# Sums of squares behind the next scores, value rows scaled last, and three PSUM banks in turn for values and tiles

## The chip, the cores and the metric

One core of a Trainium2 chip runs the program; the others are idle. The time is the device time of one execution in microseconds. Less is better.

## What is computed

Two transformer blocks on 1024 rows of width 1024, in float32. Only the first block's projections and attentions matter here; the gates, the feed-forward layer and the whole second block stay as they are.

```python
h = rms_norm(x, norm_mix[l])
aq, ak, av, bq, bk, bv, cq = jnp.split(h @ w_in[l], offsets, axis=-1)
aq = rms_norm(aq.reshape(b, t, A_HEADS, 2, A_HEAD_DIM), a_q_norm[l])
ak = rms_norm(ak.reshape(b, t, A_HEADS, 2, A_HEAD_DIM), a_k_norm[l])
...
out_a = diff_attention(aq, ak, av, slopes_a, lam)   # p[0] - lam * p[1], times v
out_a = (rms_norm(out_a, a_subln[l]) * (1.0 - lambda_init)).reshape(b, t, BRANCH_WIDTH)
...
out_c = memory_attention(cq, ck, cv)
```

So a query or key row is divided by the root of the mean of its squares, per head: 64 columns in attention A, 128 in B and C. The rows of attention A's values are normalised in the same way.

## The kernel before

**How the program is made.** Python code on the host walks through the computation once and records pieces of work in one list with `emit(kind, r)`. Then each engine walks through the whole list and issues its own share of every piece, in the order of the list. So the place at which something is emitted sets its place in the queue of every engine that has a share in it. Waits between engines are semaphores: a piece waits for the signals that its record names.

**TensorE's banks.** PSUM has eight banks. A `Banks` object gives out its banks in turn; a matmul series waits until the last user of its bank has been read out (`s_drainedN` for bank N). In attention A: scores use banks 2, 3, 4 (`SB`), transposes 5 and 6 (`TB`), projection tiles 0 and 1 (`DB`), values 7 (`OB`).

**A projection tile** is 128 rows by 256 columns: 24 matmuls (L1871), each float32 product being made of three products of split halves. For query and key tiles `qk_evac` then emits: a copy of the tile out of PSUM by DVE (L2208), the square by ACT (L1978), the sum of the squares by DVE (`TENSOR_REDUCE`, L2212), the reciprocal root by POOL (L2404, L2407), and, up to three tiles later (`QK_LAG`), the scaling by DVE (L2218, `qk_scale`), two transposes by TensorE (L1877, `qk_turn`) and the write to its place by ACT (L1986, `qk_out`). `qk_early` at the start of a step emits the scaling of all waiting tiles but the last.

**The stages** of the first block: the head (memory rows, x rows, first query and key tiles) to about 101 us, attention C to 211 us, attention A to 564 us, attention B to about 1140 us. Each attention is a pipeline of steps, written by `Att.steps`. Attention A has 32 units (4 heads by 8 blocks of 128 queries). A step of A holds the value product of the unit two steps and one back, then in alternation the scores of unit i in two halves (`scores`, L1909; 8 matmuls of 256 columns into two banks each), the transposes of the probabilities of unit i-2 (L1877 with `aE`), and DVE's part: four drains of the scores (L2232, which add the bias and keep the row maximum), three small ones (L2249, L2250, L2252) on unit i-1 (`lam_ratio`), and the mix of its two softmax halves (L2256, `lam_mix`). In the middle of the step the value rows are squared by ACT (L2015), get their reciprocal root from POOL and are scaled by DVE (L2275, `post_norm`). Last come one or two projection tiles of a later head (11, 12, 12 and 8 tiles in the four heads; 4 tiles a step once the scores are through), and the transpose of the scaled value rows of the step before (`fin_T`).

POOL also splits some weights into halves (L2397, L2399), DVE others (L2110).

Attention B works in the same way with 8 units for each of 4 heads and values in bank 7 too; its value rows are scaled by `post_plain` (L2271).

Of the kernel before, what the change touches and what calls it, by code (L numbers as in the profile page):

```python
# [201 lines left out]
def build(nc, d):  # L202
# [7 lines left out]
    with ctx:  # L210
# [47 lines left out]
        SB = Banks(every, (2, 3, 4))  # L258
        TB_TWO, TB_THREE = Banks(every, (5, 6)), Banks(every, (4, 5, 6))
        TB = TB_TWO  # L260
        OB = Banks(every, (7,))
        SB2 = Banks(every, (2, 3))
        OB2 = Banks(every, (4, 7))
        DB_FOUR = Banks(every, (0, 1, 4, 7))
# [280 lines left out]
        def qk_scratch(bufs):  # L545
            for z in range(QK):
                qk_sq[z], qk_n[z] = bufs[2 * z][:, :], bufs[2 * z + 1][:, :]

        def qk_scale(q):
            if not q.scaled:  # L550
                q.scaled = signal("qk_scaled")
                emit("qk_scale", q)
# [11 lines left out]

        def qk_evac(t, place, dh, outs, done):

            late = qk_late.pop(0) if len(qk_late) == QK_LAG else None
            if late:
                qk_turn(late)
            q = Rec()  # L570
            q.z = qk_i[0] % QK
            qk_i[0] += 1
            q.dh, q.nseg, q.place, q.outs, q.done = dh, 256 // dh, place, outs, done
            q.sq, q.nb, q.nb_free, q.sq_free = qk_sq[q.z], qk_n[q.z], flat(qk_n_free[q.z]), flat(qk_sq_free[q.z])
            q.scaled = None
            ss = stat(q.nseg)
            emit("qk_copy", q)
            if late:
                qk_out(late)
            q.squared = signal("qk_squared")  # L580
            rstd(q, ss, dh, signal("qk_summed"))
            qk_sq_free[q.z] = q.summed
            emit("qk_sq", q)
            qk_late.append(q)

        def late_turn():
# [27 lines left out]
        class Att:  # L614
# [112 lines left out]
            def steps(self, units, lag_t, fill=None, fill_n=0, lag_v=1):  # L727
                n = len(units)
                for i in range(n + lag_t + lag_v + 1):
                    qk_early()  # L730
                    unit = lambda k: units[k] if 0 <= k < n else None
                    last = unit(i - lag_t - lag_v)
                    if last and self.paired and not last.mate:
                        last = None
                    if last:
                        (self.pair_values if self.paired else self.values)(last)
                    scored = [unit(i)]
                    if self.together and self.paired:
                        scored = [unit(i), unit(i + 1)] if i % 2 == 0 else [None]
                    turns = [stage(*us) for stage, us in ((self.scores, scored), (self.probs, [unit(i - lag_t)]), (self.combine, [unit(i - 1)])) if us[0]]  # L740
                    while turns:
                        for g in list(turns):
                            if next(g, 0) == 0:
                                turns.remove(g)
                        if last:
                            last.post(self, last)
                            last = None
                    if last:
                        last.post(self, last)
                    if fill is not None:  # L750
                        for _ in range(fill_n(i) if callable(fill_n) else fill_n):
                            next(fill, None)
                    last = unit(i - lag_t - lag_v - 1)
                    if last and last.finish:
                        last.finish(self, last)
                    yield
# [4 lines left out]
        def unit(comps, ready, scale, nblk, ew, V, post, finish, btok=None, vready=(), v_at=None):  # L761
            u = Rec()
            u.comps, u.ready, u.scale, u.nblk, u.ew, u.V = comps, ready, scale, nblk, ew, V
            u.post, u.finish, u.btok, u.vready, u.v_at = post, finish, flat(btok), list(vready), v_at
            u.ocol, u.mate, u.begin, u.after, u.oT_free, u.og = 0, None, None, None, [], None
            return u

        def comp(col_, pieces):
# [12 lines left out]
        def post_norm(self, u):  # L781
            rstd(u, stat(1), 128, signal("o_squared"))
            u.oi, u.o, u.O_free = self.O.take()
            emit("post_norm", u)

        def fin_T(self, u):
            u.f_place = TB.take()
# [69 lines left out]
        aO = [rest(f"aO{i}", [128], F, 64 * KB + 15360 + 512 * i) for i in range(3)]  # L857

        c_free, c_read = [], []
        attA = Att([x[:, :] for x in aE], [x[:, :] for x in aPT], [x[:, :] for x in aO], SB, OB, dve_turns=False, together=True)  # L860
        for s_ in (attA.E, attA.PT, attA.O):
            s_.free = [c_free if s_ is attA.PT else c_read for _ in s_.bufs]
        a_units = []
# [107 lines left out]
            units, lag_t=2, lag_v=2, fill=c_fill, fill_n=lambda i: 1 if i < 6 or 11 <= i < 29 else 0)  # L971
        drain(c_fill)
        c_read[:] = [units[-1].fin, units[-1].v_full]
        c_free[:] = [c_read, t_outC]
        fillB = projB(0)
        oA_free = [[c_free], [c_free]]
# [119 lines left out]
        osp = []  # L1096
        gate_gen = gates()
        TB = TB_THREE
        attB = Att([x[:, :] for x in bE], [x[:, :] for x in bPT], [x[:, :] for x in bO], SB2, OB)
        for s_ in (attB.E, attB.PT, attB.O):  # L1100
            s_.free = [list(a_done) for _ in s_.bufs]
        b_free = a_done
# [850 lines left out]
        def _(e):  # L1953
            w = Waits(e, semaphore("act_step"))
            for kind, r in work:
# [14 lines left out]
                elif kind == "small":  # L1970
                    w.wait_ge(*w.last)
                    w.wait_ge(*lam_sum)
                    e.activation(lsum[:, 2:4], lsum[:, 0:2], ACT.Exp).then_inc(w.sig(lam_exp), 1)
                elif kind == "qk_sq":
                    w.wait_ge(*w.last)
                    w.wait_ge(*r.place.read)
                    w.wait_each(r.sq_free)
# [26 lines left out]
                elif kind == "prob" and not r.by_dve:  # L2004
# [2 lines left out]
                    w.wait_each(r.u.PT_free)  # L2007
                    dst = r.u.PT[:, r.q0 * 128:(r.q0 + r.k) * 128]
                    e.activation(dst, r.place.ps[:, 0:r.k * 128], ACT.Copy).then_inc(w.sig(r.place.read), 1)
                elif kind == "post_norm":  # L2010
                    w.wait_ge(*w.last)
                    w.wait_ge(*r.v_place.full)
                    w.wait_each(r.O_free)
# [88 lines left out]
        def _(e):  # L2102
# [70 lines left out]
            for kind, r in work:  # L2173
# [30 lines left out]
                elif kind == "qk_copy":  # L2204
# [1 line left out]
                    w.wait_ge(*r.place.full)  # L2206
                    w.wait_each(r.nb_free)
                    e.tensor_copy(r.nb, r.place.ps[:, 0:256]).then_inc(w.sig(r.place.read), 1)  # L2208
                elif kind == "qk_sq":
                    w.wait_ge(*w.last)  # L2210
                    w.wait_ge(*r.squared)
                    e.tensor_reduce(r.ss, r.sq.rearrange("p (s c) -> p s c", c=r.dh), AX.X, ALU.add).then_inc(w.sig(r.summed), 1)  # L2212
# [175 lines left out]
        def _(e):  # L2388
            w = Waits(e, semaphore("pool_step"))
            for kind, r in work:  # L2390
                if kind == "half_neg":
                    e.memset(half_neg, -0.5).then_inc(w.sig(t_hn), 1)
                elif kind == "w_split" and r.by_pool:
                    w.wait_ge(*w.last)
                    w.wait_ge(*r.loaded)
                    w.wait_each(r.free)
                    e.tensor_copy(r.hi, r.raw).then_inc(w.inner(), 1)  # L2397
                    w.wait_ge(*w.last)
                    e.tensor_tensor(r.lo, r.raw, r.hi.bitcast(F), ALU.subtract).then_inc(w.sig(r.lo_done), 1)  # L2399
                elif kind in ("row_sq", "qk_sq", "post_norm", "ln_stats"):  # L2400
                    n = r.ss.shape[-1]
                    w.wait_ge(*w.last)
                    w.wait_ge(*r.summed)
                    e.tensor_scalar(r.ss, r.ss, 1.0 / r.ss_n, EPS, ALU.mult, ALU.add).then_inc(w.inner(), 1)  # L2404
                    w.wait_ge(*w.last)
                    w.wait_ge(*t_hn)
                    e.tensor_tensor(r.ss, r.ss, half_neg[:, 0:n], ALU.pow).then_inc(w.sig(r.rstd), 1)  # L2407
                elif kind == "kr":
                    w.wait_ge(*w.last)
                    w.wait_each(kr_free)  # L2410
                    e.memset(kr96[:, :, 0:64], 0.0).then_inc(w.sig(kr_set), 1)
# [86 lines left out]
```

## Time and profile before

| what | us |
|---|---|
| median of 3 runs | 3349.6 (3348.51 to 3350.84) |
| the profiled execution | 3350.52 |
| its span, first to last instruction | 3348.1 |
| TensorE busy | 3235.5 (97%) |
| VectorE (DVE) busy | 1528.3 (46%) |
| ScalarE (ACT) busy | 1200.3 (36%) |
| GpSimd (POOL) busy | 544.7 (16%) |
| mean granted TensorE clock | 0.993 |

In the profile L12 is line 12 of the kernel. A row of a timeline is start, duration, engine, line, operation, out<-in, shapes and count; in brackets stands how long the engine was idle ahead of it, and what it waited for. In a list of waits stands who waited for whom. A window's row gives its length, the busy time of the engine, and the granted clock, 1.00 being full speed. Matmuls overlap: their durations add up to more than the time that they take.

### The profile page before, as it was taken

Reading aid. Unit: us, or ns where it says so; the run is one execution under the profiler, and the core shown is the slowest. Engines: PE = TensorE matmul, PEld = TensorE weight load, DVE = VectorE, ACT = ScalarE, POOL = GpSimd, SP = SyncE. Lnnn points to the kernel's source line nnn. Section 1 sums busy time; section 2 is a strip of 40 time slices with the busy share of each in tenths; the row PEclk is TensorE's granted clock in tenths of the full one; section 3 lists DMA queues with packets and bytes.
Section 4 is the critical chain, followed back from the end, with each engine's and each line's share of the span. In section 5 each row is a group of like instructions: output and inputs, shape, how many; then the busy total and the mean of one; then the engine's idle time right before and its main releaser. Section 6 shows DMA issues by size and latency. Waiting matters only on the chain.

```text
span 3348.1 us, 50281 instructions
## 1 busy us (share of the span) xinstructions
PE 3235.5 (97%) x19424; PEld 2745.5 (82%) x19424; DVE 1528.3 (46%) x3325; ACT 1200.3 (36%) x2325; POOL 544.7 (16%) x802
## 2 busy tenths in 40 slices
PE   6999999999999999999999999999999999999998
PEld 6978888899989888888888888888977777687776
DVE  6556565244333413334433323335344566753775
ACT  5445554333333312223221111113333555523451
POOL 3423334252523000000000000000001110023231
PEclk9999999999999999999999999999999999999999
DMA  4110001010101212112111111112200000122012
GB/s 174 52 45 17 33 20 45 26 55 26 54 26 45 80 54 73 48 54 107 38 63 49 40 51 51 51 63 88 90 34 22 15 26 14 56 90 85 26 52 100
DMA packets 32350, 178.98 MB, mean 53 GB/s; under 512 B 3697, under 2 KB 3825, under 8 KB 19697
## 3 DMA queue, kind: packets, MB, share of 16 engines
q1 hardware_dynamic: 32112, 175.78, 14.9%
q8 instruction: 154, 2.52, 0.3%
q14 instruction: 84, 0.68, 0.1%
HBM read 156.37 MB, written 19.40 MB: 52 GB/s over the span
## 4 chain that ended last, share of the span: by engine, by line
PE 77%; DVE 4%; ACT 2%; issue 2%; POOL 0%; DMA 0%; DVEq 0%; ACTq 0%; SPq 0%; POOLq 0%
PE ps L1871 64%; PE ps L1909 4%; PE ps L1877 4%; PE ps L1930 2%; PE ps L1922 2%; PE ps L1933 1%; PE ps L1950 1%; ACT aE L2003 0%; DVE aE L2232 0%; DVE wlo L2110 0%; DVE mPT L2263 0%; DVE rt L2115 0%; DVE cols L2115 0%; POOL xlo_ln L2399 0%; DVE mE L2232 0%
## 5 line engine op out<-in xcount | busy, mean ns | idle before, releaser
L1871 PE MATMUL ps<-hhi,whi 128*128 128x512 f32 x1568 | 617.2, 394 | 0.0
L1871 PE MATMUL ps<-hhi,wlo 128*128 128x512 f32 x1568 | 611.4, 390 | 0.0
L1871 PE MATMUL ps<-hlo,whi 128*128 128x512 f32 x1568 | 610.8, 390 | 0.0
L1871 PE MATMUL ps<-whi,hhi 128*128 128x256 f32 (+2 forms) x1920 | 581.1, 303 | 2.0 <-ACT z L1993 1.7
L1871 PE MATMUL ps<-wlo,hhi 128*128 128x256 f32 (+2 forms) x1920 | 565.3, 294 | 0.0
L1871 PE MATMUL ps<-whi,hlo 128*128 128x256 f32 (+2 forms) x1920 | 565.3, 294 | 0.0
L2404 POOL TENSOR_SCALAR stats<-stats 128x2 f32<-128x2 f32 (+2 forms) x230 | 68.0, 296 | 2182.5 <-ACT jk L1964 810.5
L1871 PEld LDWEIGHTS ps<-whi,hhi 128*128 128x128 f32 x1920 | 368.8, 192 | 11.3 <-ACT z L1993 1.9
L1871 PEld LDWEIGHTS ps<-wlo,hhi 128*128 128x128 f32 x1920 | 369.3, 192 | 7.9 <-issue 0.2
L1871 PEld LDWEIGHTS ps<-whi,hlo 128*128 128x128 f32 x1920 | 368.6, 192 | 7.6
L1871 PEld LDWEIGHTS ps<-hhi,wlo 128*128 128x128 f32 x1568 | 294.5, 188 | 62.0
L1871 PEld LDWEIGHTS ps<-hhi,whi 128*128 128x128 f32 x1568 | 294.7, 188 | 59.8 <-issue 0.7
L1871 PEld LDWEIGHTS ps<-hlo,whi 128*128 128x128 f32 x1568 | 294.8, 188 | 59.6
L1960 ACT ACTIVATE whi<-raw 128x1024 fp32r<-128x1024 f32 (+2 forms) x158 | 155.1, 981 | 290.8 <-PE ps L1871 284.2
L2110 DVE TENSOR_TENSOR wlo<-raw,whi 128x1024 fp32r<-128x1024 f32 (+2 forms) x158 | 177.9, 1126 | 177.3 <-ACT whi L1960 174.5
L2399 POOL TENSOR_TENSOR wlo<-raw,whi 128x512 fp32r<-128x512 f32 (+4 forms) x164 | 204.7, 1248 | 13.1
L2397 POOL CAST whi<-raw 128x512 fp32r<-128x512 f32 (+4 forms) x164 | 96.2, 587 | 573.1 <-PE ps L1871 564.0
L2407 POOL TENSOR_TENSOR stats<-stats 128x2 f32<-128x2 f32 (+2 forms) x230 | 164.8, 716 | 19.2
L2300 DVE TENSOR_TENSOR x<-ps,x 128x512 f32<-128x512 f32 x112 | 77.5, 692 | 160.8 <-PE ps L1871 159.9
L2212 DVE TENSOR_REDUCE stats<-qk 128x2 f32<-128x256 f32 (+1 forms) x148 | 62.2, 420 | 176.0 <-ACT qk L1978 176.0
L1871 PE MATMUL ps<-whi,fhi 128*128 128x512 f32 x352 | 137.7, 391 | 0.0
L1871 PE MATMUL ps<-whi,flo 128*128 128x512 f32 x352 | 137.2, 390 | 0.0
(340 smaller groups left out, 5417.5 us busy)
## 6 DMA issues: line engine op xcount, KB each, us to landing
raw<-in_W SPq DMA_DIRECT2D x93, 1024.0 KB, 4.9
raw<-in_W SPq DMA_DIRECT2D x24, 768.0 KB, 4.2
orw<-scratch_outs SPq DMA_DIRECT2D x3, 2048.0 KB, 7.7
xin<-in_x SPq DMA_DIRECT2D x8, 512.0 KB, 14.4
x<-in_x SPq DMA_DIRECT2D x8, 512.0 KB, 7.1
scratch_x<-x SPq DMA_DIRECT2D x8, 512.0 KB, 3.8
x1b<-scratch_x SPq DMA_DIRECT2D x8, 512.0 KB, 7.2
scratch_h<-x1b SPq DMA_DIRECT2D x8, 512.0 KB, 4.2
```

The lines of the kernel that those rows point to most:

```text
L1871: x = e.matmul(r.out, a, b, start=(r.start and m == 0), stop=(r.stop and m == n - 1))
L1877: x = e.transpose(place.ps[0:rows, j * 128:(j + 1) * 128], b, ident[:, :])
L1909: x = e.matmul(p.place.ps[:, o:o + n], *p.blocks[b], start=True, stop=True)
L1922: x = e.matmul(r.v_place.ps[:, 0:r.ew], r.PT[:, j * 128:(j + 1) * 128], r.V[j], start=(j == 0), stop=(j == r.nblk - 1))
L1930: x = e.matmul(r.v_place.ps[64 * s:64 * s + 64, 0:128], u.V[j], u.PT[:, j * 128:(j + 1) * 128], start=(j == 0), stop=(j == r.nblk - 1))
L1960: e.activation(r.hi, r.raw, ACT.Copy).then_inc(w.sig(r.hi_done), 1)
L2110: e.tensor_tensor(r.lo, src, r.hi.bitcast(F), ALU.subtract).then_inc(w.sig(r.lo_done), 1)
L2300: e.tensor_tensor(r.o, r.place.ps[:, :], r.o, ALU.add).then_inc(w.sig(r.place.read), 1)
L2397: e.tensor_copy(r.hi, r.raw).then_inc(w.inner(), 1)
L2399: e.tensor_tensor(r.lo, r.raw, r.hi.bitcast(F), ALU.subtract).then_inc(w.sig(r.lo_done), 1)
L2404: e.tensor_scalar(r.ss, r.ss, 1.0 / r.ss_n, EPS, ALU.mult, ALU.add).then_inc(w.inner(), 1)
L2407: e.tensor_tensor(r.ss, r.ss, half_neg[:, 0:n], ALU.pow).then_inc(w.sig(r.rstd), 1)
```

## The change

It has three parts. First, `qk_evac` no longer emits the sum of the squares at once but keeps it in a list; `qk_sums` emits what is in the list. It is called at the next `qk_evac`, by `qk_scale` if the tile to be scaled is in the list, and in every step of every attention after the first round of scores, turns and ratios. Second, `post_norm` is taken apart: ACT's square and POOL's root stay where they were (`o_square`), the scaling by DVE is emitted after the scores, turns and mix of the step, ahead of the projection tiles (`u.later`). Third, attention A's and B's values and, from attention A on, the projection tiles share the banks 0, 1 and 7 in turn.

```diff
-        OB = Banks(every, (7,))
+        DB_OB = Banks(every, (0, 1, 7))
...
+        qk_unsummed = []
+
+        def qk_sums():
+
+            while qk_unsummed:
+                q = qk_unsummed.pop(0)
+                rstd(q, q.ss, q.dh, signal("qk_summed"))
+                qk_sq_free[q.z] = q.summed
+                emit("qk_sum", q)
+
         def qk_scale(q):
+            if q in qk_unsummed:
+                qk_sums()
             if not q.scaled:
...
         def qk_evac(t, place, dh, outs, done):
 
+            qk_sums()
             late = qk_late.pop(0) if len(qk_late) == QK_LAG else None
...
-            q.squared = signal("qk_squared")
-            rstd(q, ss, dh, signal("qk_summed"))
-            qk_sq_free[q.z] = q.summed
-            emit("qk_sq", q)
+            q.squared, q.ss = signal("qk_squared"), ss
+            emit("qk_square", q)
+            qk_unsummed.append(q)
             qk_late.append(q)
...
                         for g in list(turns):
                             if next(g, 0) == 0:
                                 turns.remove(g)
+                        qk_sums()
                         if last:
                             last.post(self, last)
                             last = None
                     if last:
                         last.post(self, last)
+                    valued = unit(i - lag_t - lag_v)
+                    if valued and valued.later:
+                        valued.later()
                     if fill is not None:
...
             rstd(u, stat(1), 128, signal("o_squared"))
             u.oi, u.o, u.O_free = self.O.take()
-            emit("post_norm", u)
+            emit("o_square", u)
+            u.later = lambda: emit("post_norm", u)
...
-        attA = Att([x[:, :] for x in aE], [x[:, :] for x in aPT], [x[:, :] for x in aO], SB, OB, dve_turns=False, together=True)
+        attA = Att([x[:, :] for x in aE], [x[:, :] for x in aPT], [x[:, :] for x in aO], SB, DB_OB, dve_turns=False, together=True)
...
         c_read[:] = [units[-1].fin, units[-1].v_full]
+        DB = DB_OB
...
-        attB = Att([x[:, :] for x in bE], [x[:, :] for x in bPT], [x[:, :] for x in bO], SB2, OB)
+        attB = Att([x[:, :] for x in bE], [x[:, :] for x in bPT], [x[:, :] for x in bO], SB2, DB_OB)
```

The branches of the engines' loops follow: ACT's `qk_sq` and `post_norm` become `qk_square` and `o_square`, DVE's `qk_sq` becomes `qk_sum`, and POOL's root hangs on `qk_sum` and `o_square`. The lines of the engines' code move down by 18 (L2212 is L2230 after, L2275 is L2293).

DVE in attention A, a step with one tile, before. `aE` are the scores, `qk` with an even number a tile's copy and with an odd one its squares, `aO` the value rows.

```order
293 L2256 SCALAR_TENSOR_TENSOR aE_110<-aE_110,stats 128x1024
294 L2208 COPY qk_92<-ps 128x256
295 L2212 TENSOR_REDUCE stats<-qk_91 128x4
296 L2218 TENSOR_TENSOR qk_98<-qk_98,stats 128x256
297 L2232 ISA aE_109,stats<-ps,atab 128x512
298 L2232 ISA stats 128x1
299 L2232 ISA aE_109,stats<-ps,atab 128x512
300 L2232 ISA stats 128x1
301 L2249 RECIPROCAL stats<-stats 128x1
302 L2250 RECIPROCAL stats<-stats 128x1
303 L2252 SCALAR_TENSOR_TENSOR stats<-stats 128x1
304 L2275 TENSOR_SCALAR aO_115<-ps,stats 128x128
```

The same place with the change:

```order
292 L2274 SCALAR_TENSOR_TENSOR aE_110<-aE_110,stats 128x1024
293 L2293 TENSOR_SCALAR aO_114<-ps,stats 128x128
294 L2226 COPY qk_92<-ps 128x256
295 L2236 TENSOR_TENSOR qk_98<-qk_98,stats 128x256
296 L2250 ISA aE_109,stats<-ps,atab 128x512
297 L2250 ISA stats 128x1
298 L2250 ISA aE_109,stats<-ps,atab 128x512
299 L2250 ISA stats 128x1
300 L2267 RECIPROCAL stats<-stats 128x1
301 L2268 RECIPROCAL stats<-stats 128x1
302 L2270 SCALAR_TENSOR_TENSOR stats<-stats 128x1
303 L2230 TENSOR_REDUCE stats<-qk_91 128x4
```

The sum has changed places with the value rows: it stood between copy and scaling and now stands behind the first two drains, and the value rows have gone behind the mix.

DVE in the head, before. `wlo` is a weight split, `xsc` a scaled row block of x, `hlo` a split of its transpose.

```order
17 L2110 TENSOR_TENSOR wlo_57<-raw_53,whi_55 128x1024
18 L2208 COPY qk_94<-ps 128x256
19 L2212 TENSOR_REDUCE stats<-qk_93 128x2
20 L2182 SCALAR_TENSOR_TENSOR xsc_70<-xin_60,stats,gb_69 128x1024
21 L2110 TENSOR_TENSOR wlo_56<-raw_52,whi_54 128x1024
22 L2208 COPY qk_96<-ps 128x256
23 L2212 TENSOR_REDUCE stats<-qk_95 128x2
24 L2187 TENSOR_TENSOR hlo<-ps,hhi 128x4x128 x2
25 L2182 SCALAR_TENSOR_TENSOR xsc_71<-xin_61,stats,gb_69 128x1024
26 L2110 TENSOR_TENSOR wlo_56<-raw_52,whi_54 128x1024
27 L2218 TENSOR_TENSOR qk_92<-qk_92,stats 128x256
```

With the change:

```order
16 L2128 TENSOR_TENSOR wlo_57<-raw_53,whi_55 128x1024
17 L2230 TENSOR_REDUCE stats<-qk_91 128x2
18 L2226 COPY qk_94<-ps 128x256
19 L2200 SCALAR_TENSOR_TENSOR xsc_70<-xin_60,stats,gb_69 128x1024
20 L2128 TENSOR_TENSOR wlo_56<-raw_52,whi_54 128x1024
21 L2230 TENSOR_REDUCE stats<-qk_93 128x2
22 L2226 COPY qk_96<-ps 128x256
23 L2205 TENSOR_TENSOR hlo<-ps,hhi 128x4x128 x2
24 L2200 SCALAR_TENSOR_TENSOR xsc_71<-xin_61,stats,gb_69 128x1024
25 L2128 TENSOR_TENSOR wlo_56<-raw_52,whi_54 128x1024
26 L2230 TENSOR_REDUCE stats<-qk_95 128x2
27 L2236 TENSOR_TENSOR qk_92<-qk_92,stats 128x256
```

Each sum has moved from behind the copy of its tile to behind the weight split that follows; the sum of `qk_95` now stands directly ahead of the scaling of `qk_92`.

TensorE, values, scores and next tile in a step of A, before and with the change: only the banks differ.

```order
1502 L1922 MATMUL ps<-aV_104,aPT_112 128x128 [waits s_drained7]
1503 L1922 MATMUL ps<-aV_104,aPT_112 128x128 x7
1504 L1909 MATMUL ps<-ak_102,aq_100 128x256 [waits s_drained4,s_drained3]
...
1508 L1909 MATMUL ps<-ak_102,aq_100 128x256 [waits s_drained3,s_drained2]
...
1512 L1871 MATMUL ps<-whi_55,hhi 128x256 [waits s_drained1]
```

```order
1502 L1940 MATMUL ps<-aV_104,aPT_112 128x128 [waits s_drained1]
1503 L1940 MATMUL ps<-aV_104,aPT_112 128x128 x7
1504 L1927 MATMUL ps<-ak_102,aq_100 128x256 [waits s_drained4,s_drained3]
...
1508 L1927 MATMUL ps<-ak_102,aq_100 128x256 [waits s_drained3,s_drained2]
...
1512 L1889 MATMUL ps<-whi_55,hhi 128x256 [waits s_drained7]
```

The values now wait for the release of bank 1 and the tile for that of bank 7; the scores' banks are the same.

## Rows read from the trace of the kernel before

**Rows 1.** Waits of TensorE, 210 to 700 us: us in total, times, longest.
```profile
PE ps L1909 <- DVE stats L2232: 28.4, 34, 2.1
...
PE ps L1877 <- DVE aO L2275: 2.6, 1, 2.6
```

**Rows 2.** TensorE by group: form, xcount | busy us, mean ns | idle us before, releaser.
```profile
L1909 PE MATMUL ps<-ak,aq 64*128 64x256 f32 x512 | 73.3, 404 | 27.7 <-DVE stats L2232 27.7
```

**Rows 3.** Timeline of TensorE, two steps of A: start us, us, instruction [idle before].
```profile
313.21 1.14 PE L1909 MATMUL ps<-ak,aq 64*128 64x256 f32 x8
...
315.31 1.14 PE L1909 MATMUL ps<-ak,aq 64*128 64x256 f32 x8 [0.38 <-DVE stats L2232]
...
321.95 1.13 PE L1909 MATMUL ps<-ak,aq 64*128 64x256 f32 x8
...
325.07 1.13 PE L1909 MATMUL ps<-ak,aq 64*128 64x256 f32 x8 [1.40 <-DVE stats L2232]
```

**Rows 4.** Timeline of DVE, the same two steps.
```profile
314.47 0.69 DVE L2232 CUSTOM_DVE_ANT_1 aE<-ps,atab 128x512 f32<-128x512 f32 x1 [0.39 <-PE ps L1909]
...
317.22 0.41 DVE L2275 TENSOR_SCALAR aO<-ps,stats 128x128 f32<-128x128 f32 x1 [0.57 <-POOL stats L2407]
...
319.51 1.29 DVE L2256 SCALAR_TENSOR_TENSOR aE<-aE,stats 128x1024 f32<-128x1024 f32 x1
320.83 0.42 DVE L2208 COPY qk<-ps 128x256 f32<-128x256 f32 x1
323.31 0.42 DVE L2212 TENSOR_REDUCE stats<-qk 128x4 f32<-128x256 f32 x1 [2.05 <-ACT qk L1978]
323.76 0.43 DVE L2218 TENSOR_TENSOR qk<-qk,stats 128x256 f32<-128x256 f32 x1
324.22 0.69 DVE L2232 CUSTOM_DVE_ANT_1 aE<-ps,atab 128x512 f32<-128x512 f32 x1
```

**Rows 5.** Waits of DVE, 213 to 560 us: us in total, times, longest.
```profile
DVE stats L2212 <- ACT qk L1978: 62.1, 39, 2.2
...
DVE aO L2275 <- POOL stats L2407: 9.5, 13, 1.9
```

**Rows 6.** Timeline of TensorE, first steps of A, and a window: us, busy, clock, DMA, GB/s.
```profile
213.46 1.14 PE L1909 MATMUL ps<-ak,aq 64*128 64x256 f32 x8 [0.89 <-DVE stats L2232]
...
217.58 1.13 PE L1909 MATMUL ps<-ak,aq 64*128 64x256 f32 x8
220.81 1.84 PE L1909 MATMUL ps<-ak,aq 64*128 64x256 f32 x8 [2.10 <-DVE stats L2232]
...
226.49 1.13 PE L1909 MATMUL ps<-ak,aq 64*128 64x256 f32 x8
...
220.00:224.00 4.00, 3.19 (x14) 0.64 0.01 4
```

**Rows 7.** TensorE, DVE and POOL near 352 us, and the window behind.
```profile
352.89 0.41 PE L1877 MATMUL ps<-ident,qk 128*128 128x128 f32 x2 [2.67 <-DVE qk L2218]
...
349.93 1.41 DVE L2256 SCALAR_TENSOR_TENSOR aE<-aE,stats 128x1024 f32<-128x1024 f32 x1
351.37 1.38 DVE L2218 TENSOR_TENSOR qk<-qk,stats 128x256 f32<-128x256 f32 x1
...
350.33 2.13 POOL L2399 TENSOR_TENSOR wlo<-raw,whi 128x512 fp32r<-128x512 f32 x1
...
352.00:356.00 4.00, 3.11 (x20) 0.78 0.66 203
```

**Rows 8.** TensorE, last values of attention B (three such rows).
```profile
1133.56 2.28 PE L1922 MATMUL ps<-bV,bPT 128*128 128x128 f32 x18 [0.32 <-DVE bO L2271]
```

**Rows 9.** Head: DVE and TensorE.
```profile
24.65 0.42 DVE L2212 TENSOR_REDUCE stats<-qk 128x2 f32<-128x256 f32 x1 [0.61 <-ACT qk L1978]
...
38.59 0.42 DVE L2218 TENSOR_TENSOR qk<-qk,stats 128x256 f32<-128x256 f32 x1
...
39.16 0.41 PE L1877 MATMUL ps<-ident,qk 128*128 128x128 f32 x2 [4.08 <-DVE qk L2218]
```

More of the change, by code:

```diff
@@ L764, in unit @@
             u.post, u.finish, u.btok, u.vready, u.v_at = post, finish, flat(btok), list(vready), v_at
-            u.ocol, u.mate, u.begin, u.after, u.oT_free, u.og = 0, None, None, None, [], None
+            u.ocol, u.mate, u.begin, u.after, u.later, u.oT_free, u.og = 0, None, None, None, None, [], None
             return u
@@ L1973, in _ @@
                     e.activation(lsum[:, 2:4], lsum[:, 0:2], ACT.Exp).then_inc(w.sig(lam_exp), 1)
-                elif kind == "qk_sq":
+                elif kind == "qk_square":
                     w.wait_ge(*w.last)
@@ L2009, in _ @@
                     e.activation(dst, r.place.ps[:, 0:r.k * 128], ACT.Copy).then_inc(w.sig(r.place.read), 1)
-                elif kind == "post_norm":
+                elif kind == "o_square":
                     w.wait_ge(*w.last)
@@ L2208, in _ @@
                     e.tensor_copy(r.nb, r.place.ps[:, 0:256]).then_inc(w.sig(r.place.read), 1)
-                elif kind == "qk_sq":
+                elif kind == "qk_sum":
                     w.wait_ge(*w.last)
@@ L2399, in _ @@
                     e.tensor_tensor(r.lo, r.raw, r.hi.bitcast(F), ALU.subtract).then_inc(w.sig(r.lo_done), 1)
-                elif kind in ("row_sq", "qk_sq", "post_norm", "ln_stats"):
+                elif kind in ("row_sq", "qk_sum", "o_square", "ln_stats"):
                     n = r.ss.shape[-1]
```

## The prediction

> **What bounds the kernel now.** I read the list of waits of TensorE first, since it is the one engine that is nearly always busy (3235.5 of 3348.1 us), so that only its idle time and its clock can be won. In 210 to 700 us, the stretch that the change works on, one wait stands out: scores that wait for DVE, 28.4 us in 34 waits; what follows is single waits, such as the 2.6 us at the end of attention A [rows 1]. The grouped instructions say whose wait that is: the scores of attention A (512 matmuls, 32 steps of two halves of 8) have 27.7 us of idle time before them, all put down to the DVE operation that drains scores out of PSUM [rows 2]. The timeline shows the pattern. The first half never waits in a way that matters; the second half waits until DVE has drained the first bank of the first half, since the three score banks hold only one half and a half. In some steps that wait is 0.38 us, in others 1.40 us [rows 3]. The DVE rows of the same two steps say why [rows 4]. Where DVE had nothing left to do, the first drain started 0.39 us after it went idle, at 314.47, that is 1.26 us after the half's first matmul. Where a projection tile had been copied at the end of the step before, DVE stood at 323.31 in the sum of squares, 2.05 us behind ACT's square, then did the scaling of an older tile (323.76) and came to the drain at 324.22, that is 2.27 us after the matmuls began (321.95): 1.01 us later. 1.40 less 0.38 is 1.02 us. The list of waits of DVE has the cause as one line: 39 sums that wait 62.1 us for ACT's squares; value rows wait 9.5 us for POOL [rows 5].
>
> **The change, part by part.** Nothing is added or removed on an engine; only DVE and POOL get another order, and TensorE other banks.
>
> *Sums behind the next scores' drains.* The 2.05 us wait disappears from the place ahead of the first drain. What stays ahead of it is mix, value scaling, copy and scaling of the old tile: from 319.51 that is 1.32 + 0.45 + 0.45 + 0.46 = 2.7 us, done at 322.2, and the scores' first bank is full at 323.2 (321.95 + 1.26). So the first drain is set by TensorE itself and the second half starts 2.10 us after the first, as at 313.21 and 315.31. The floor of the wait is then 0.38 us in 30 steps. The first two have no transposes between the halves and show 0.89 us where nothing disturbs them [rows 6]; I take 0.89 for both. 30 x 0.38 + 2 x 0.89 = 13.2 us remain of 27.7: **-14.5 us**. No row shows less than 0.38 us, so it is also the most that this can give; nothing, if the drains are held by something else, is a rival below.
>
> Does DVE have the time? In a step with one tile it works from 314.47 to 321.25 but for 0.57 us of waiting, plus 0.91 us of sum and scaling [rows 4]: 7.1 us. The step took 9.76 us from half to half (315.31 to 325.07) and should take 8.74. 1.6 us of slack is left.
>
> *The clock.* The second step of A has the largest of these waits, 2.10 us at 220.81, and behind it 8 scores take 1.84 us for 1.14, and the matmuls stay slow until 224.4; the granted clock of 220 to 224 is 0.64 [rows 6], that is, part of it at the lower of the two levels, 1.2 instead of 2.4 GHz. From the second half to the next first half, the same instructions took 4.12 us the first time (213.46 to 217.58) and 5.68 us the second (220.81 to 226.49). With 0.89 us instead of 2.10 ahead of it I expect no fall: **-1.5 us** (bounds 0 and -1.6).
>
> *Value rows last in a step.* In the steps without a copied tile this scaling stood between the drains and waited for POOL: 0.57 us at 317.22 [rows 4], and in all 9.5 us in 13 waits. Nobody on TensorE waits for those second drains (the next scores come 6 us later), so this is worth nothing by itself, except that mix comes up to 1.1 us earlier. That matters at one place. At 352.89 two transposes of a late tile waited 2.67 us for a DVE scaling that took 1.38 us instead of 0.43, beside a POOL split of 2.13 us [rows 7]. Mix ahead of it now starts near 348.8 instead of 349.93, value scaling adds 0.45, and the scaling starts near 350.6 instead of 351.37. If it is then held until the POOL piece that began at 350.33 ends after its usual 1.3 us, it ends at 352.0 instead of 352.75: **-0.8 us**. That the two hold each other up is in the rows: 1.38 and 2.13 us together, 0.43 and 1.30 us where they meet nothing. If nothing holds it, it is -1.7 us, and the granted clock behind the wait, 0.78 in 352 to 356 and not up again before 360, stays up too: about 1.4 us more, -3.1. If all stays behind POOL as now, 0. The Trainium skill (SBUF — State Buffer, "Who interferes with whom") speaks for this last end: a DVE operation with two SBUF inputs and a GpSimd operation that reads SBUF exclude one another for a whole instruction, and the one that issued first goes on. By that rule mix, which has two such inputs, would at 348.8 fall into the POOL piece of 348.28 and stand until 349.6, and the whole sum would be -14.9 us instead of the one below.
>
> *Three banks in turn.* Attention A's values had bank 7 to themselves and tiles banks 0 and 1; now both take 0, 1, 7 in turn. A tile's bank comes free by a DVE copy, a value's by value scaling, one to two takes back. In a step with one tile a bank is taken again three takes, one and a half steps (13 us), later, and the value scaling, behind the next mix, some 9 us after the values began (the next mix ends near 329, a step behind the one at 319.51 [rows 4]). In a step with two tiles (11.8 us) the next values take the bank of the last values, about 2.5 us after that scaling. I cost this at nothing; what covers it is those 2.5 us, and if they are gone each us of lateness is one of TensorE's. At the end of attention B the values waited 0.33, 0.32 and 0.41 us for the release of the one value bank [rows 8]; with three banks that goes: **-1.0 us** (bounds 0 and -1.1). The boundary from A to B keeps their 2.6 us wait [rows 1].
>
> *The head.* The same postponement works before 101 us, where DVE has less time to spare. There a sum waited 0.61 us for ACT and then ran while DVE had time; now it stands behind the weight split that follows, and its own 0.42 to 0.46 us is added to a chain that is full. Three such sums lie ahead of the scaling at 38.59, for which TensorE waited 4.08 us, and one ahead of each of the next two such scalings [rows 9]. 3 x 0.45 less the little that a saved wait gives back is +1.2 us, and 2 x 0.45 at the two: **+2.1 us** (bounds 0, if the removed waits of 0.61 us pay for it, and +4, if the 4.08 us wait also brings a longer stretch at the low clock). In attention C and in B the sums move behind other small DVE work that TensorE does not wait for: 0.
>
> Sum: -14.5 - 1.5 - 0.8 - 1.0 + 2.1 = -15.7 us. The profiled execution took 3350.5 us, 0.9 over the median of 3349.6 us. 3350.5 - 15.7 = 3334.8; against the median 3333.9 us.
>
> **Rivals.** *The change does what it says, but DVE has less slack than I count* (the tail of a step, mix to scaling, is 2.7 us and any collision with POOL, as the 1.38 for 0.43 us above, adds up to 0.95 us to it). Against it stands the slack of 1.6 us and the 1.0 us between 322.2 and 323.2; for it, that steps with two tiles have a second copy behind the last matmul of the second tile, just before the next step. If half of the waits come back as later drains it is -7.2 in place of -14.5, -8.4 in all, and 3341 us.
>
> *Nothing shows:* the drains are held by something else, e.g. ACT, which frees the E buffers with its exponentials, or the second wait was never DVE's order. Against it: in the undisturbed steps the wait is 0.38 us with the same ACT and PE rows. What is left is -0.8 - 1.0 + 2.1: 3350 us.
>
> *Slower:* POOL's queue. A value's reciprocal root now stands behind the tile's, and both behind weight pieces of 0.6 + 1.3 us (up to 2.1). Value scaling is no longer in the middle of a step but ahead of copy and scaling; if its root comes late, everything behind it on DVE is late: the copy (that frees a tile's bank), the scaling (for which TensorE's transposes wait) and the next drains. It decides from the point at which the lateness exceeds the 1.6 us of slack, and a root that is queued behind two splits is 2 x 1.9 us late: 2.2 us over, in the 12 or so steps of a stretch with weight splits +26 us less the 15.7: about 3360 us. For it: 13 waits of this kind exist now. Against it: they are 0.7 us in the mean, and the scaling moves back by 3.4 us (from 317.22 past 320.83), which is more than their longest, 1.9 us.
>
> **How the numbers follow.** My case 0.70, half of it 0.18, nothing 0.07, slower 0.05. The likeliest gives 3334 us; its bounds together reach from -20.3 (3329.3) to -10.5 (3339.1). With the case of half the gain and its own bounds the range is **3329.5 to 3342.5 us**. 0.2% of 3349.6 is 6.7 us, about what a measurement of this kernel can tell from no change; so faster means under 3342.9. My case and nearly all of the half case lie there: faster 0.85, same 0.10, slower 0.05.
>
> **What would show it.** In the profile after, the idle time before A's scores is about 13 us (27.7 now), nearly each second half with 0.38 us; sums on DVE no longer have a wait of 2 us, and stand behind the ratio of the two softmax sums; the clock of the second step of A does not fall; the wait at 39.16 grows by 1.2 us to 5.3. Wrong would be: many second halves still at 1 us and over (DVE's tail), a new wait of values or of a tile's first matmul for a bank, value scaling waiting for POOL longer than now, or a TensorE wait for a scaled tile in each step.

## The result, and the profile after

The changed kernel took 3332.0 us (median of 4 runs, 3331.3 to 3338.3) beside 3350.2 us for the kernel before (median of 4 runs, 3348.5 to 3351.4). The ratio is 0.9950, 95% interval 0.9933 to 0.9967, so 18.2 us less. Forecast were 3334.0 us, 3329.5 to 3342.5, and faster with a chance of 0.85.

The profiled execution took 3332.6 us, its span is 3330.2 us, 17.9 less than before. TensorE is busy for 3232.1 us. The group of A's scores among the grouped instructions, and the waits of TensorE in 210 to 700 us (us in total, times, longest), answering to [rows 1, 2]:

```profile
L1927 PE MATMUL ps<-ak,aq 64*128 64x256 f32 x512 | 72.6, 400 | 14.3 <-DVE stats L2250 14.3
```

```profile
PE ps L1927 <- DVE stats L2250: 15.0, 34, 1.4
PE ps L1895 <- DVE aO L2293: 2.1, 1, 2.1
```

14.3 us of idle time are left of 27.7; 13.2 were forecast. The wait of the transposes for the value rows at the end of A is 2.1 us instead of 2.6. Of the 32 second halves, 29 now wait 0.38 us; the first three wait 0.89, 0.98 and 1.44. TensorE in two such steps, answering to [rows 3]:

```profile
317.89 1.14 PE L1927 MATMUL ps<-ak,aq 64*128 64x256 f32 x8
...
319.99 1.14 PE L1927 MATMUL ps<-ak,aq 64*128 64x256 f32 x8 [0.38 <-DVE stats L2250]
```

DVE beside them, answering to [rows 4]:

```profile
312.62 0.42 DVE L2230 TENSOR_REDUCE stats<-qk 128x4 f32<-128x256 f32 x1
313.07 0.69 DVE L2250 CUSTOM_DVE_ANT_1 aE<-ps,atab 128x512 f32<-128x512 f32 x1
...
316.24 0.41 DVE L2293 TENSOR_SCALAR aO<-ps,stats 128x128 f32<-128x128 f32 x1
316.68 0.42 DVE L2226 COPY qk<-ps 128x256 f32<-128x256 f32 x1
317.14 0.42 DVE L2236 TENSOR_TENSOR qk<-qk,stats 128x256 f32<-128x256 f32 x1
319.14 0.69 DVE L2250 CUSTOM_DVE_ANT_1 aE<-ps,atab 128x512 f32<-128x512 f32 x1 [1.58 <-PE ps L1927]
```

The sum runs ahead of the second pair of drains without a wait, the value rows are scaled ahead of the copy, and DVE is done 1.58 us before the first drain can begin. That idle time is the spare time that the forecast had put at 1.6 us.

Where the 17.9 us lie can be told by placing the same instructions of TensorE in both traces beside one another; after minus before is +2.5 us where A begins, -14.8 us where it is over, -15.4 us at 1550 us, -15.5 us at 2550 us and -18.0 us at the end. So the head lost 2.5, attention A gave 17.3, the rest of the first block gave 0.6, and the last 2.5 us come from the second block, in which nothing was changed. Forecast were +2.1 for the head, -16.8 for A, -1.0 for B and nothing for the second block.

### The profile page after: what moved, and what is told of

It is laid out like the page before. It is cut to its first block, busy times and chain, and to the rows that moved or that the text cites. A ratio compares the mean times of both kernels' runs of the same rounds, so it can differ in the third digit from the quotient of the medians.

```text
span 3330.2 us, 50291 instructions
## 1 busy us (share of the span) xinstructions
PE 3232.1 (97%) x19424; PEld 2743.9 (82%) x19424; DVE 1544.3 (46%) x3325; ACT 1201.3 (36%) x2325; POOL 545.2 (16%) x802
## 4 chain that ended last, share of the span: by engine, by line
PE 90%; DVE 5%; issue 2%; ACT 2%; DMA 0%; POOL 0%; DVEq 0%; SPq 0%; ACTq 0%; POOLq 0%
PE ps L1889 70%; PE ps L1927 7%; PE ps L1895 6%; PE ps L1940 4%; PE ps L1948 2%; PE ps L1951 1%; DVE wlo L2128 1%; PE ps L1968 1%; ACT whi L1978 0%; DVE mPT L2281 0%; DVE aE L2250 0%; DMA raw<-in_W 0%; DVE qk L2236 0%; DVE rt L2133 0%; DVE cols L2133 0%
## 5 line engine op out<-in xcount | busy, mean ns | idle before, releaser
L2422 POOL TENSOR_SCALAR stats<-stats 128x2 f32<-128x2 f32 (+2 forms) x230 | 61.0, 265 | 2157.8 <-ACT jk L1982 810.3
L1889 PEld LDWEIGHTS ps<-whi,hhi 128*128 128x128 f32 x1920 | 368.3, 192 | 10.8 <-ACT z L2011 1.7
L2415 POOL CAST whi<-raw 128x512 fp32r<-128x512 f32 (+4 forms) x164 | 106.6, 650 | 579.4 <-PE ps L1889 570.3
L1889 PE MATMUL ps<-wlo,fhi 128*128 128x512 f32 x352 | 136.9, 389 | 0.0
```

The lines of the kernel that those rows point to most:

```text
L1889: x = e.matmul(r.out, a, b, start=(r.start and m == 0), stop=(r.stop and m == n - 1))
```

## Experiments

All are compared with the kernel before, run on the same chip between them (medians 3350.0, 3350.3 and 3350.4 us). "In A" is how much less or more time TensorE took between the begin and the end of attention A than in the profile before, from the traces placed beside one another; in the changed kernel it is -17.3 us. Each diff is against the changed kernel and cut to the lines that the text is about; where a run builds on another one, what it has from that one is left out.

### One part at a time

e1, the sums alone; on the changed kernel:

```diff
-            u.later = lambda: emit("post_norm", u)
+            emit("post_norm", u)
-        DB_OB = Banks(every, (0, 1, 7))
+        OB = Banks(every, (7,))
...
-        DB = DB_OB
```

(and `attA` and `attB` take `OB` again).

> Only the sums are postponed; value rows are scaled in the middle of the step and the banks are those of before. Theory (the three parts need each other): the value's root now stands behind the tile's on POOL, so value scaling, still ahead of the second drains on DVE, comes about 2.5 us later; DVE's work and wait in a step with one tile come to 7.1 + 2.5 = 9.6 us, more than the 8.74 us of TensorE, so the waits of the second halves come back as waits for late drains: 3344 to 3351 us, idle time before A's scores over 22 us. Rival (the sum's place alone makes the gain): idle time about 14 us, 3332 to 3336 us.

Measured: 3373.2 us, ratio 1.0070 (1.0058 to 1.0083), in A +20.8 us. The rival falls. The theory had the cause, value scaling that waits for POOL, and missed the size: the time is more than 20 us over its range. DVE's waits in 205 to 565 us, and those of TensorE:

```profile
DVE aO L2292 <- POOL stats L2424: 64.1, 30, 2.9
```

```profile
PE ps L1894 <- ACT ak L2003: 18.0, 10, 2.0
PE ps L1894 <- ACT bk L2003: 10.9, 8, 2.2
PE ps L1926 <- DVE stats L2249: 10.4, 18, 1.4
```

DVE waits 64.1 us for the value's root (9.5 us before, [rows 5]). And the time does not come back at the place that the theory named: the second halves wait for only 10.4 us, but the first transposes of the probabilities wait 28.9 us for ACT, where that wait had been 0.9 us in all. How that comes about is shown by e5 and e9. All these waits are about 11 us more than before. The rest is for the most part the clock: in A it is at the low level for a while seven times instead of twice, six times right behind a wait of 2.0 us or more. One such window (us, busy, clock, DMA share, GB/s):

```profile
260.00:264.00 4.00, 4.00 (x20) 0.58 0.02 6
```

At some 1.4 us each, the price near 352 us below, five more of them are about 7 us; this is an estimate.

e2, value rows last and shared banks, but each sum at once behind its copy:

```diff
             qk_unsummed.append(q)
+            qk_sums()
```

> Only the value rows are scaled last and the banks shared; each sum follows the copy of its tile at once, as before. Theory: DVE still stands in the sum behind ACT's square ahead of the first drain, so the idle time before A's scores stays at 26 to 28 us and the second step of A keeps its 2.1 us wait and its slow clock; what goes is the wait near 352 us (1.3 to 2.7 us) and the values' waits at the end of B (1.1 us): 3346 to 3348 us. Rival (the wait for POOL in the middle of the step was the true cause): idle time under 18 us, about 3336 us.

Measured: 3338.1 us, ratio 0.9962 (0.9950 to 0.9975), in A -10.8 us. This is neither of the two forecasts, and the most telling run: without its headline part the change already gives 12 us. The scores, and DVE's wait for the squares:

```profile
L1928 PE MATMUL ps<-ak,aq 64*128 64x256 f32 x512 | 73.3, 403 | 18.9 <-DVE stats L2251 18.9
```

```profile
DVE stats L2231 <- ACT qk L1997: 52.0, 41, 1.7
```

The sums still wait for ACT, but the second halves that waited for 0.98 us wait for 0.53, those with 1.39 for about 0.41, while the first steps keep 2.10, 1.24 and 1.11. So the square came earlier, because the value scaling no longer stands ahead of the second drains. What went is its 0.41 us and, in the steps with 1.39, the 0.57 us that it had waited for POOL as well [rows 4]; so the rival was right in part. DVE and ACT form a loop: second drains of the scores, two exponentials, two writes of a turned tile, square, sum, next first drain. ACT in one such step of e2:

```profile
461.15 1.16 ACT L2022 ACTIVATE aE<-aE,stats 128x1024 f32<-128x1024 f32 x1 [0.67 <-DVE stats L2256]
...
462.43 1.15 ACT L2022 ACTIVATE aE<-aE,stats 128x1024 f32<-128x1024 f32 x1
...
463.75 0.37 ACT L2005 ACTIVATE bq<-ps,cols 128x128 f32<-128x128 f32 x1
464.15 0.49 ACT L2005 ACTIVATE bk<-ps,cols 128x128 f32<-128x128 f32 x1
464.67 0.42 ACT L1997 ACTIVATE qk<-qk 128x256 f32<-128x256 f32 x1
```

ACT works with hardly a gap from the end of the second drains (461.15) to the end of the square (465.09): 3.9 us, so each us by which the drains come earlier is an us for the sum, until the first drain waits for TensorE.

e3, the banks alone (each sum at once, as in e2, and the value scaling in the middle of the step, as in e1):

> Only the three shared banks. Theory: nothing but the 1.1 us of the values at the end of B: 3348.5 to 3350 us, idle time before A's scores 27 to 28 us. Rival (a bank that comes free late costs in A): 3351 us and over, with waits of values or of tiles' first matmuls for a bank in A.

Measured: 3347.4 us (11 runs, 3344.8 to 3351.9), ratio 0.9992 (0.9983 to 1.0001). In A nothing moves (28.5 us of waits for the drains, 28.4 before), and the values of B lose their wait. The theory holds for both, except that B gave 2.6 us in the trace and not 1.1; the median is a little under its range, and the interval just includes no difference.

e7, the whole change with values in bank 7 alone:

```diff
-        DB_OB = Banks(every, (0, 1, 7))
+        OB = Banks(every, (7,))
...
-        DB = DB_OB
```

> The whole change without the shared banks: values in bank 7 alone. Theory (the banks are needed for the late value scaling): the next values wait for it, 0.7 to 0.8 us in each of 21 steps with one tile, little in those with two: 3343 to 3352 us, with a wait of the value matmuls for DVE aO of 15 us in all. Rival (the banks carry nothing but the 1.1 us at the end of B): 3331 to 3335 us.

Measured: 3349.0 us, ratio 0.9999 (0.9990 to 1.0009), in A -3.8 us. The scores still wait for only 14.3 us, and the rest has gone into this:

```profile
PE ps L1939 <- DVE aO L2292: 10.8, 19, 1.0
```

The late value scaling needs the shared banks: 19 values wait for it, 10.8 us (15 were expected), of the 13.5 us lost in A. A wait costs more than its own length here: from value product to value product a step takes 9.54 us (479.12 to 488.66, with a wait of 0.54), where it took 8.73 in the changed kernel. So the banks are worth next to nothing alone (e3) and 17 us together with the rest (3349.0 against 3332.0). The late scaling alone, with one value bank and the sums in their old place, was not run.

### Does it matter where the sum stands?

e5 is e1 with the postponed sum behind the value scaling:

```diff
-                        qk_sums()
                         if last:
                             last.post(self, last)
                             last = None
+                        qk_sums()
```

> As e1 (sums postponed, value rows scaled in the middle of the step, banks of before), but a step's postponed sum is emitted behind the value scaling instead of ahead of it, on DVE and on POOL. Theory (e1 lost its time because the value's root stood behind the tile's root on POOL and DVE waited 2.2 us for it in each step, 64 us in all): the wait for POOL is back at 0.6 us, the second drains start about as early as in the kernel before, the loop of DVE drains, ACT exponentials and squares no longer holds the first drain: idle time before A's scores 12 to 17 us, 3334 to 3340 us. Rival (postponed sums cost by themselves, wherever they stand in the middle of a step): over 3360 us.

Measured: 3349.3 us (10 runs), ratio 0.9995 (0.9986 to 1.0005), in A -6.2 us. Changing the sum's place behind the value's took back 23.9 us, all that e1 had lost, so the order of the two, and with it that of their roots on POOL, was its cause; but the forecast of 3334 to 3340 is missed. DVE still waits for POOL (31.8 us, 32 times) and has the sum of 0.42 us to do besides between its two pairs of drains. TensorE in a step of e5:

```profile
476.94 1.13 PE L1926 MATMUL ps<-ak,aq 64*128 64x256 f32 x8
478.72 0.66 PE L1894 MATMUL ps<-ident,aE 128*128 128x128 f32 x4 [0.64 <-ACT bk L2003]
```

The wait has moved from the second half of the scores to the transposes of the probabilities ahead of it. They go into the bank of the last turned tile, which ACT reads after its two exponentials, and these begin after the second drains.

e4, the change with sums postponed in A alone:

```diff
             qk_unsummed.append(q)
+            if not in_A[0]:
+                qk_sums()
...
+        in_A[0] = True
         attA.run(a_units, lag_t=2, lag_v=1, fill=a_fill, fill_n=a_fill_n)
         drain(a_fill)
+        in_A[0] = False
+        qk_sums()
```

> The whole change, but sums are postponed in attention A alone; in the head, in attentions C and B each sum follows its copy at once. Theory: the head's loss of 2.7 us and the small losses in B (three waits of a turn for its scaling, about 0.65 us each, four longer waits for boT, 0.23 us each) go, A keeps its gain: 3326.5 to 3329.5 us. Rival (the head's difference is the granted clock's chance and not the sums' place): 3331 to 3333 us.

Measured: 3330.2 us, ratio 0.9940 (0.9927 to 0.9952). In A -17.3 us, as in the changed kernel; where A begins the trace is 0.2 us behind that of before instead of 2.5. The medians differ by 1.7 us, and 3330.2 lies between the two forecasts; the traces by stages decide it. In the four profiles with sums postponed in the head (the change, e1, e5, e7) attention A begins 1.7 to 2.5 us later than before, in the seven others between 1.2 us earlier and 0.9 us later. So the loss in the head is the sums' place and no chance.

e10, with the next experiment's order of transposes, and A's sums behind the mix:

```diff
-                        qk_sums()
                         if last:
...
+                    qk_sums()
                     valued = unit(i - lag_t - lag_v)
```

> e6 with the sums of A behind the mix, ahead of the value scaling, so that no extra DVE work stands between the two pairs of drains. Theory (in e6 TensorE waits for nothing in the steps of A any more, so drains that come 0.45 us earlier give it nothing): as e6, 3317 to 3321 us. Rival (the early drains free ACT and DVE in steps with two tiles, where a few waits are left): 1 to 2 us less.

Measured: 3326.8 us, ratio 0.9927 (0.9914 to 0.9939), in A -18.3 us; the time is 7.8 us more than that of e6. Both forecasts are wrong. DVE's waits:

```profile
DVE qk L2243 <- POOL stats L2432: 23.4, 26, 3.3
```

These were 7.7 us in 9 waits in e6. A sum that comes some 3 us later gets its root from POOL later, and the scaling at the next step's begin, ahead of the first drain, waits for it. In the longest of these waits the sum was done at 233.66, four pieces of weight splits kept POOL until 237.60, and the root came at 238.98. So there is a place too late for the sum as well.

### How much time do DVE and ACT have?

e8, e4 with five copies of a tile instead of one in A, 1.8 us more between mix and scaling:

```diff
+                    for _ in range(4 if r.again else 0):
+                        inner(lambda: e.tensor_copy(r.nb, r.place.ps[:, 0:256]))
...
                     e.tensor_copy(r.nb, r.place.ps[:, 0:256]).then_inc(w.sig(r.place.read), 1)
```

> e4 with each copy of a query or key tile in A made five times over by DVE, so 1.8 us more of DVE work in a step with one tile, between mix and scaling. Theory (DVE has 1.6 us of slack there, as the wait of the first drain for TensorE shows, 1.57 us): the first drains of these steps come only 0.2 to 0.4 us late, more in the steps with two tiles, whose second copy is the last thing before the drains: 3333 to 3345 us. Rival (DVE has no slack, each us on it is one of the kernel): 3330 + 31 tiles x 1.8 us = 3386 us.

Measured: 3353.1 us (10 runs), ratio 1.0010 (1.0000 to 1.0019), in A +7.2 us; 22.8 us over e4, and neither forecast. In most steps with one tile the second half waits for 0.67 to 0.69 us, 0.3 us more than the floor, as 1.8 less 1.58 us of spare time would have it. In the steps with two tiles it waits for 1.28 to 1.72 us, about 1 us more, and behind the first steps' 2.18 and 2.58 us the slow clock is back (0.63 in 220 to 224 us, 0.66 in 232 to 236). So the spare time of 1.6 us is real in steps with one tile; those with two have about half of it, and there the forecast range was too low.

e9, e4 with each sum in A made four times, 1.35 us more between the pairs of drains:

```diff
+                    for _ in range(3 if r.again else 0):
+                        inner(lambda: e.tensor_reduce(r.ss, r.sq.rearrange("p (s c) -> p s c", c=r.dh), AX.X, ALU.add))
```

> e4 with each sum in A made four times over by DVE, so 1.35 us more of DVE work between the first and the second pair of drains. Theory (what delays the second drains reaches TensorE through ACT: the exponentials start later, then the writes of the last tile's transposes, whose bank the first group of probability transposes waits for): the spare time there is 0.65 us (ACT ends at 462.09, the transposes are due at 462.74 in the profile of the change), so these transposes wait 0.6 to 0.8 us in each step with a tile, the second halves less than 0.38, net 0.3 to 0.5 us a step: 3338 to 3346 us. Rival (only DVE's own spare time of 1.57 us ahead of the first drain counts, and 1.35 us fit into it): 3329 to 3333 us with no such waits.

Measured: 3354.3 us (10 runs), ratio 1.0010 (1.0000 to 1.0019), in A +6.5 us; 24.1 us over e4. TensorE in a step with one tile, and its waits in 205 to 565 us:

```profile
476.80 1.13 PE L1933 MATMUL ps<-ak,aq 64*128 64x256 f32 x8
478.60 0.66 PE L1901 MATMUL ps<-ident,aE 128*128 128x128 f32 x4 [0.67 <-ACT bk L2010]
479.45 1.14 PE L1933 MATMUL ps<-ak,aq 64*128 64x256 f32 x8 [0.19 <-DVE stats L2260]
```

```profile
PE ps L1933 <- DVE stats L2260: 18.0, 24, 1.7
PE ps L1901 <- ACT ak L2010: 6.4, 14, 0.6
PE ps L1901 <- ACT bk L2010: 5.9, 8, 1.7
```

The mechanism is as the theory had it: 0.67 + 0.19 us where the floor is 0.38, a loss of 0.48 us a step. The total is larger than the range, since the steps with two tiles wait for up to 1.73 us for late first drains as well, and a stretch of slow clock came back (0.61 in 228 to 232 us).

### A version that beats both

e6, e4 with both groups of A's probability transposes between the two halves of the scores:

```diff
                     emit("prob", r)
                     u.pt_read.append(r.place.read)
-                    yield
+                    if not in_A[0] or q0:
+                        yield
```

> e4 (the change with sums postponed in A alone), and in A both groups of four transposes of probabilities stand between the two halves of the scores on TensorE, where one group stood between and one behind. Theory: the floor of 0.38 us in each step is the time by which the first drain's bank comes free after 8 scores and 4 transposes; 4 more transposes, 0.42 us, fill it: idle time before A's scores under 4 us, 3317 to 3322 us. Rival (the second group waits for its bank, which ACT reads last for aoT, so one wait takes the place of the other): a new wait of L1895 for ACT aoT of 0.3 us a step, 3327 to 3330 us.

Measured: 3319.1 us (3317.6 to 3323.2), ratio 0.9910 (0.9895 to 0.9925); in A -27.7 us. The scores:

```profile
L1934 PE MATMUL ps<-ak,aq 64*128 64x256 f32 x512 | 72.6, 401 | 3.1 <-DVE stats L2257 2.9
```

The floor of 0.38 us was no property of the drain but of what TensorE was given to do meanwhile; 29 of the 32 second halves now wait for nothing. The wait of the second group for its bank did not come. 31 us under the kernel before, 13 under the change.

## Why the prediction was right, and where it was not

*Sums behind the next drains, -14.5 us.* The idle time fell by 13.4 us to 14.3, against a floor of 13.2 that was counted; the excess is in the second and third steps, 0.98 and 1.44 us. The place, the size and the floor were right. What the term claimed besides was wrong: that the sum's place does this. e1 and e2 show that the sum alone costs 20.8 us in A, that the two other parts without it give 10.8 us, and that the sum adds 6.5 us to them.

*"Value rows last in a step ... worth nothing by itself."* This is the step that failed. I looked at who waits for the second drains on TensorE, found the next scores 6 us later, and stopped. ACT waits for them, and TensorE waits for ACT at the transposes, or DVE does at the sum. The term was about 8 to 9 us of the 13.4 (18.9 us of idle time are left in e2), and it stood under another heading. The total was right because the forecast took the floor for the whole change, and the floor does not ask which part reaches it; as far as the parts go, that was luck.

*The clock, -1.5 us.* Right at its place: the second step of A now waits for 0.98 us instead of 2.10, and the granted clock stays up. But a new slow stretch stands at the end of A, behind the 2.09 us wait for the value rows, and took 1.5 us back. The windows' rows, answering to [rows 6]:

```profile
220.00:224.00 4.00, 3.02 (x23) 1.00 0.02 4
548.00:552.00 4.00, 4.00 (x24) 0.57 0.39 97
```

*The turn near 352 us, -0.8 us (0 to -3.1).* It gave 2.65 us: the wait is 1.39 us instead of 2.67 [rows 7], and the slow clock behind it is gone, 1.38 us. TensorE, DVE and POOL there:

```profile
346.54 0.41 PE L1895 MATMUL ps<-ident,qk 128*128 128x128 f32 x2 [1.39 <-DVE qk L2236]
```

```profile
343.77 1.72 DVE L2274 SCALAR_TENSOR_TENSOR aE<-aE,stats 128x1024 f32<-128x1024 f32 x1
345.53 0.41 DVE L2293 TENSOR_SCALAR aO<-ps,stats 128x128 f32<-128x128 f32 x1
345.97 0.42 DVE L2236 TENSOR_TENSOR qk<-qk,stats 128x256 f32<-128x256 f32 x1
```

```profile
343.12 1.30 POOL L2417 TENSOR_TENSOR wlo<-raw,whi 128x512 fp32r<-128x512 f32 x1
344.48 1.48 POOL L2415 CAST whi<-raw 128x512 fp32r<-128x512 f32 x1
346.04 1.50 POOL L2417 TENSOR_TENSOR wlo<-raw,whi 128x512 fp32r<-128x512 f32 x1
```

The mix did meet the POOL piece, took 1.72 us instead of 1.28, and POOL's next piece took 1.48 instead of 0.61. That is the direction of the Trainium skill's rule (SBUF — State Buffer, "Who interferes with whom"), a DVE operation with two SBUF inputs and a GpSimd operation that reads SBUF in each other's way, and the value scaling, which reads PSUM, took its usual 0.41 us beside the 1.48 us piece. Its size is nearly right too. The mix came 0.65 us before the end of the POOL piece that had been issued first, so by the rule it would have lost 0.65 us, and it lost 0.44. The scaling kept its 0.42 us because it was issued 0.07 us ahead of POOL's next piece, which took 1.50 us instead of 1.30. What my use of the rule left out is that the mix held POOL up in turn: the POOL piece issued beside it ended 0.87 us late, and so the split behind it, which before had held the scaling, was issued only after the scaling.

*Three banks, -1.0 us.* The three waits of 1.06 us at the end of B are gone, as forecast, and the values of A never wait. The trace gained 1.85 us there, since each of these waits had cost about 0.6 us; with what the banks gave earlier in B it is 2.6 us in e3. "I cost this at nothing" was right with the late scaling, but e7 shows what hung on it: 17 us.

*The head, +2.1 us.* It was +2.5. The scaling for which TensorE waits came at 39.78 instead of 38.59, 1.19 us later (about 1.2 counted):

```profile
39.32 0.42 DVE L2230 TENSOR_REDUCE stats<-qk 128x2 f32<-128x256 f32 x1
39.78 0.42 DVE L2236 TENSOR_TENSOR qk<-qk,stats 128x256 f32<-128x256 f32 x1
```

But DVE was not full there: it waited 1.56 us for a weight half and 1.24 us for a half of x's transpose, both from ACT, whose squares came later because each sum now stood ahead of a tile's copy. The wait ahead of the scaling did not grow to 5.3 us, as forecast, but was 3.95, since TensorE itself came later: its clock was 0.65 in 28 to 32 us, where it had been 1.00.

*"In attention C and in B ... 0."* Too simple. In B three turns now wait 0.39 us for a scaling, which cost about 0.6 us each; the same three stand in e1, which has no shared banks. Four waits for ACT's `boT` are 0.90 us instead of 0.67, but so they are in e3, so they belong to the banks and not to the sums. Between the end of A and the last head of B the trace lost 1.2 us net, before the banks gave 1.85.

*The second block.* 2.5 us came from stretches of slow clock that are as old as the kernel and were shorter this time, with the same work and the same waits; windows of before and after:

```profile
2872.00:2884.00 12.00, 9.42 (x28) 0.72 0.25 88
```

```profile
2855.00:2867.00 12.00, 9.41 (x36) 0.86 0.25 88
```

In the ten other runs' profiles the second block, just as unchanged, took between 1.9 us less and 2.9 us more than before. So some 2.5 us of the gain in the profile are not the change's, and one profile of this kernel tells no more finely than that.

*Rivals.* Of the slower one, POOL's queue, the mechanism exists: it is e1. It did not strike in the change since the value scaling had moved back by 3.1 us (4.99 us behind the start of the second half, 311.25 to 316.24, where it had been 1.91), which is the argument given against it, with 3.4. The DVE tail did not cost anything: 1.58 us were left in a step with one tile.

## What to carry over

Follow a delayed instruction through every engine that waits for it, and not only to the bottleneck's next wait: a DVE operation of 0.4 us that "nobody on TensorE waits for" was, with its own waits for POOL, worth some 9 us here (e2 against e3), through two exponentials, a square and a bank that ACT frees. Parts of a change can be worth nothing or less alone and much together (the sums +23 us alone, the banks -2.6, banks and late scaling -12, all three -18), so a failed single edit is not proof against the idea. And a wait floor is often set by the work that stands beside it: the 0.38 us in each step went away by moving 4 transposes.

## What the runs showed of the hardware

The granted clock falls behind a wait of TensorE in some runs and not in others: the wait of 2.09 us at the end of A was followed by 0.57 in 548 to 552 us in the changed kernel, the one of 2.65 us at the same place before by none. And when the DVE mix of 1.28 us was issued while a POOL piece ran (343.77), it grew by 0.44 us, and the POOL piece issued while the mix ran (344.48) grew by 0.87 us; the one that had been there first kept its 1.30 us.
